# Output projection walked by halves of the tokens, with the second norm and the first dense products interleaved

## What is computed

```
for l in range(2):
    x = x + mod[2] * (concat(attention, conv, rwkv, fourier) @ w_out[l])   # the output projection
    h = modulate(rms_norm(x, norm2_w[l]), mod[3], mod[4])                  # the second norm
    if l == 0:   # dense block, 22 tiles of 128 hidden channels
        x = x + mod[5] * ((silu(h @ w1) * (h @ w3)) @ w2)
    else:        # router, top 2 of 8 experts
        x = x + mod[5] * moe_swiglu(h, router_w, w1, w3, w2)
```

## Time and profile before

| | |
|---|---|
| time, median of 2 runs | 2254.22 us (2253.96 to 2254.49) |
| the profiled execution: its time | 2271.23 us |
| its span | 2269.0 us, so 2.2 us lie around it |
| mean granted TensorE clock | 0.956 |
| TensorE busy | 2093.4 us, 92% |
| VectorE / ScalarE / GpSimd busy | 53% / 31% / 12% |

### The profile page before, as it was taken

One profiled execution on the slowest core, in us unless ns is written; L12 is line 12 of the kernel. 1 busy time (PEld: TensorE's weight loads), 2 busy tenths in 40 slices (PEclk: granted clock), 3 DMA queues, 4 the chain that ended last, 5 costly groups with the idle time before them and its releaser, 6 DMA issues.

```text
span 2269.0 us, 48183 instructions
## 1 busy us (share of the span) xinstructions
PE 2093.4 (92%) x20626; PEld 1798.4 (79%) x20626; DVE 1202.9 (53%) x2421; ACT 694.1 (31%) x1194; POOL 265.0 (12%) x377
## 2 busy tenths in 40 slices
PE   6999788889799999999899969888969999999996
PEld 3757577786599999999666757887749999899995
DVE  3458645544466422323456864545166666666664
ACT  3010323330422122121211142342045444544542
POOL 0000214520000000000000303551000110101110
PEclk8999869999899999999999978999989999999998
DMA  8253201001134322210435301000145666656666
GB/s 301 94 204 113 77 3 43 4 5 36 40 111 149 112 75 75 75 66 30 149 103 172 107 31 41 7 4 3 38 183 185 219 218 203 210 210 220 211 200 200
DMA packets 190652, 256.51 MB, mean 113 GB/s; under 512 B 9168, under 2 KB 141728, under 8 KB 190272
## 3 DMA queue, kind: packets, MB, share of 16 engines
q1 hardware_dynamic: 185456, 237.32, 30.2%
q0 software_dynamic: 4992, 16.13, 2.9%
HBM read 239.26 MB, written 16.78 MB: 113 GB/s over the span
## 4 chain that ended last, share of the span: by engine, by line
PE 82%; DVE 8%; issue 3%; ACT 3%; DMA 2%; SPq 1%; POOL 1%; DVEq 0%; ACTq 0%; POOLq 0%
PE bank L970 41%; PE bank L961 9%; PE bank L1241 9%; PE bank L1483 6%; PE bank L944 3%; PE bank L1120 3%; PE bank L1209 2%; PE bank L1226 2%; PE bank L1197 1%; PE bank L931 1%; DMA ring<-in_moe_w 1%; DVE arena L2393 1%; ACT arena L1660 1%; DVE rms L1943 1%; DMA arena<-in_mod_w 1%
## 5 line engine op out<-in xcount | busy, mean ns | idle before, releaser
L970 PE MATMUL bank<-g_hi,w_hi 128*128 128x224 f32 (+1 forms) x1376 | 392.8, 285 | 10.2 <-issue 6.4
L970 PE MATMUL bank<-g_hi,w_lo 128*128 128x224 f32 (+1 forms) x1376 | 391.4, 284 | 0.0
L970 PE MATMUL bank<-g_lo,w_hi 128*128 128x224 f32 (+1 forms) x1376 | 391.2, 284 | 0.0
L2131 DVE TENSOR_TENSOR w_lo<-ring,w_hi 128x1024 fp32r<-128x1024 f32 x192 | 232.2, 1223 | 133.9 <-ACT w_hi L1901 133.7
L1241 PE MATMUL bank<-arena 64*64 64x64 f32 (+1 forms) x8640 | 261.6, 226 | 32.1 <-issue 19.0
L1241 PEld LDWEIGHTS bank<-arena 64*64 64x64 f32 x8640 | 245.9, 134 | 47.0 <-issue 25.3
L970 PEld LDWEIGHTS bank<-g_hi,w_hi 128*128 128x128 f32 x1376 | 264.6, 192 | 12.2 <-issue 7.2
L970 PEld LDWEIGHTS bank<-g_lo,w_hi 128*128 128x128 f32 x1376 | 264.6, 192 | 0.2
L970 PEld LDWEIGHTS bank<-g_hi,w_lo 128*128 128x128 f32 x1376 | 264.5, 192 | 0.0
L1901 ACT ACTIVATE w_hi<-ring 128x1024 fp32r<-128x1024 f32 x192 | 202.3, 1060 | 129.5 <-PE bank L970 113.8
L970 PE MATMUL bank<-h_hi,w_hi 128*128 128x320 f32 x704 | 221.2, 314 | 11.5 <-DVE h_lo L2496 11.5
(11 more groups left out here) (296 smaller groups left out, 2929.8 us busy)
## 6 DMA issues: line engine op xcount, KB each, us to landing
ring<-in_moe_w SPq DMA_DIRECT2D x100, 1024.0 KB, 7.1
arena<-in_mod_w SPq DMA_DIRECT2D x40, 1024.0 KB, 5.3
ring<-in_ffn_w SPq DMA_DIRECT2D x30, 1024.0 KB, 7.4
ring<-in_w_in SPq DMA_DIRECT2D x16, 1024.0 KB, 7.5
ring<-in_w_out SPq DMA_DIRECT2D x8, 1024.0 KB, 8.6
ring<-in_mod_w SPq DMA_DIRECT2D x8, 1024.0 KB, 6.2
ring<-in_dft SPq DMA_DIRECT2D x4, 1024.0 KB, 7.4
ring<-in_w_in SPq DMA_DIRECT2D x4, 896.0 KB, 11.0
```

The costliest lines, as they stand in the source:

```text
L970: ins = mm(out, lhs[x], rhs[y], start=(first and i == 0), stop=(last and i == 2))
L2131: v.tensor_tensor(dst[1], src, f32(dst[0]), ALU.subtract).then_inc(s_lo2, 1)
```

## The change

The projection is walked by halves: 8 tiles of half 0, then 8 tiles of half 1. The second norm is done per half. Sums of squares of half 0 (one row-group sum and one fold) stand on TensorE between the tiles of half 1; root, inversion, scaling, shift, and in layer 0 `h_hi` and `h_lo` of half 0, stand on ScalarE and VectorE between the residuals of half 1. In layer 0 the first eight product groups of the dense block (chunks 0 and 1) are ordered half 0 first, with the sums of half 1 behind the first of them, and `w_lo` of chunks 0 and 1 stands ahead of the norm of half 1. The mod sums, takes and folds of the dense block each move one chunk later. In layer 1 the router's parts are made per half, and the early transposes stand between them. The line numbers shift: L970 becomes L995, L1483 becomes L1519, L2048 becomes L2170, L2606 becomes L2713, L1974 becomes L2096.

```diff
@@ project on TensorE, both layers
-                square_parts(2, l, 2 * l + 2)
-                sum_squares(2, l)
+                for h in range(2):
+                    for dt in range(KT):
+                        g = (dt, h)
+                        if g in early:
+                            end(project(g, (4, 5)))
+                            continue
+                        if g == (4, 0):
+                            wait_item(pe, ("wout", l, 1))
+                        banks[g] = psum[order.open(pe, ("out", l, dt, h))]
+                        end(project(g, (0, 1, 2, 3, 6, 7, 4, 5)))
+                        if g == (0, 1):
+                            second_sums(l, 0)
+                        elif g == (1, 1):
+                            sum_part(2, l, 0)
...
@@ dense on TensorE
             def dense():
+                for n, (f, q, h) in enumerate(FIRST_UPS):
+                    dense_up(0, f, q, h)
+                    if n == 0:
+                        second_sums(0, 1)
+                        sum_part(2, 0, 1)
                 for p, (_, nf) in enumerate(DENSE_PARTS):
-                    for f in range(nf):
-                        n = chunk_no[(p, "up", f)]
-                        pe.wait_ge(s_lo, n + 1)
...
-                        if p == 0 and f > 0:
-                            mod_sub(1, f - 1)
+                                dense_up(p, f, q, h)
+                        if p == 0:
+                            mod_sub(1, f - 2)
...
@@ norm2 and loop over chunks on ScalarE
+                for k in range(KT):
+                    square(1, k)
+                    if 2 <= k < 6:
+                        shift(0, 2 * k - 4)
+                        shift(0, 2 * k - 3)
+                    if l == 0 and k == 6:
+                        dense_split(0)
+                if l == 0:
+                    dense_split(1)
+                    silu(0, 0, 0)
+                else:
+                    b = take(("rpart", l, 0))
+                    end(ac(rt_part[:, 0:HALF], b[:, 0:HALF], ACT.Copy))
+                root(2, l, 1)
...
                     for n, (p, kind, i) in enumerate(chunks):
-                        if n + 1 < len(chunks):
+                        if 0 < n < len(chunks) - 1:
                             dense_split(n + 1)
...
@@ norm2 on VectorE
+                    elif dt == 6:
+                        low(0, 6)
+                        low(0, 7)
+                        if l == 0:
+                            dense_split(0)
+                if l == 0:
+                    dense_split(1)
+                b = take(("sp2", l, 1))
+                end(v.tensor_copy(rs[:, HALF:TOK], b[:, 0:HALF]))
+                invert(2, l, 1)
+                chain.settle()
+                for k in range(KT):
+                    scale(k, HALF_SEGS[1])
+                    if k >= 2:
+                        low(1, k - 2)
+                low(1, KT - 2)
+                low(1, KT - 1)
...
@@ loop over chunks on VectorE
+                    for h in range(2):
+                        for i in range(2):
+                            gated(0, i, h)
                     for n, (p, kind, i) in enumerate(chunks):
-                        if n + 1 < len(chunks):
+                        if 0 < n < len(chunks) - 1:
...
+                            if u >= 2:
+                                for h in range(2):
+                                    gated(p, i, h)
                             ve.wait_ge(s_ghi, u + 1)
                             v.tensor_tensor(dg[1][:, i, :], sil[:, u % 2, :], f32(dg[0][:, i, :]), ALU.subtract).then_inc(s_glo, 1)
...
+                        if 1 < n <= SUB_FIRST + 1:
+                            mod_take(1, n - 2)
                         if 0 < n <= SUB_FIRST:
-                            mod_take(1, n - 1)
-                        if n < SUB_FIRST:
-                            mod_sums(1, n)
+                            mod_sums(1, n - 1)
```

More of the change, by code:

```diff
@@ new lines, in _ @@
+                for g in early:
+                    banks[g] = psum[order.open(pe, ("out", l, g[0], g[1]))]
+                    project(g, (0, 1, 2, 3, 6, 7))
+                for ct in range(2):
+                    for h in range(2):
+                        order.wait_emptied(pe, ("gup", l, ct, h))
+                for h in range(2):
+                    for dt in range(KT):
+                        g = (dt, h)
[10 more added lines that the diff above has]
+                            sum_part(2, l, 0)
@@ L1553, in _ @@
                             end(ins)
-                for h in range(2):
-                    order.wait_emptied(pe, ("ss2", l, h))
                 if l == 0:
@@ L1633, in take, with norm1 @@
                 return psum[order.bank(name)]
-            def norm(l, which, then=None):
-                if l == 0 and which == 1:
+            def norm1(l):
+                if l == 0:
                     for j in range(NT):
@@ L1666, in in_evac, with silu, by_token @@
+            def silu(p, i, h):
+                u = DENSE_PARTS[p][0] + i
+                b = take(("du", p, i, 0, h))
+                end(ac(sil[:, u % 2, HALF * h:HALF * (h + 1)], b[:, 0:HALF], ACT.Silu))
+            def by_token(tiles):
+                for j, q in tiles:
+                    if q == 0:
+                        b = take(("ht", j, q))
+                        end(ac(h_tok[:, j, 0:512], b[:, :], ACT.Copy))
             def in_evac(l, tiles):
@@ L1849, in _ @@
                                 act.wait_ge(s_glo, u - 1)
-                            for h in range(2):
-                                b = take(("du", p, i, 0, h))
-                                end(ac(sil[:, u % 2, HALF * h:HALF * (h + 1)], b[:, 0:HALF], ACT.Silu))
+                                for h in range(2):
+                                    silu(p, i, h)
                             if i == 0 and p > 0:
@@ L1929, in take, with scales @@
                 return psum[order.bank(name)]
-            def norm(l, which, then=None):
-                b = take((f"sp{which}", l, 1))
-                end(v.tensor_copy(rs[:, HALF:TOK], b[:, 0:HALF]))
-                if which == 1:
-                    first_mods(l)
+            def scales(l, which):
                 t = 24 * (which - 1) + 8
@@ L1940, in norm, with invert, norm1 @@
                                                  in1=w[:, :, None].broadcast_to([P, KT, 2]), op0=ALU.add, op1=ALU.mult))
+            def invert(n, l, h):
+                order.wait_emptied(ve, (f"ss{n}", l, h))
+                chain.did(v.reciprocal(rs[:, HALF * h:HALF * (h + 1)], rs[:, HALF * h:HALF * (h + 1)]))
+            def norm1(l):
+                b = take(("sp1", l, 1))
+                end(v.tensor_copy(rs[:, HALF:TOK], b[:, 0:HALF]))
+                first_mods(l)
+                scales(l, 1)
@@ L1951, in norm, with scale @@
-                    ins.then_inc(s_hmul, 1)
-                    if then and k >= 2:
-                        then(k - 2)
-                if then:
-                    then(KT - 2)
-                    then(KT - 1)
+                    scale(k, SEGS)
+            def scale(k, segs):
+                for vec, lo, hi in segs:
+                    ins = v.scalar_tensor_tensor(out=hT[:, k, lo:hi], in0=xT[:, k, lo:hi], scalar=amul[:, k, vec:vec + 1],
+                                                 in1=rs[:, lo:hi], op0=ALU.mult, op1=ALU.mult)
+                    if vec == 0:
+                        chain.did(ins)
+                ins.then_inc(s_hmul, 1)
@@ L2489, in _, with by_token @@
                         end(v.tensor_tensor(yT[:, ct, cols], b[:, 0:HALF], yT[:, ct, cols], ALU.mult))
-                for dt in range(KT):
-                    for h in range(2):
-                        end(residual(take(("out", l, dt, h)), h, dt, 16))
-                def low(k):
-                    ve.wait_ge(s_hhi, k + 1)
-                    v.tensor_tensor(hc[1][:, k, :], hT[:, k, :], f32(hc[0][:, k, :]), ALU.subtract).then_inc(s_hlo, 1)
-                if l == 0:
-                    dense_split(0)
-                    norm(l, 2, low)
-                else:
-                    norm(l, 2)
-                if l == 1:
+                norm2(l)
+                if l == 1:
+                    def by_token(tiles):
+                        for j, q in tiles:
+                            if q == 1:
+                                b = take(("ht", j, q))
+                                end(v.tensor_copy(h_tok[:, j, 512:1024], b[:, :]))
+                    by_token(HT_EARLY)
                     three = lambda x: x[:, :, None].broadcast_to([P, NT, NE])
```

273 lines of the change are left out of this document (149 added, 124 removed).

## The result

The changed kernel takes 2286.43 us (median of 2 runs, 2281.60 and 2291.26) against 2254.22 before. The measured ratio is 1.0109, with a 95% interval of 1.0068 to 1.015: slower by 1.1%, less than the 2% that this measurement can surely tell from no change, but by its interval a loss. The two medians shown, divided, give 1.0143 (32.2 us); from which runs the smaller ratio comes isn't known, and the interval holds both. The forecast was 2280, range 2262 to 2291. The profiled execution is the longer of the two: 2291.26 us, span 2289.4, which is 20.4 us over the span of before.

The account below looks back on a forecast made before the run. TensorE, busy 92% of the span, was taken as the bound, with the load ring near the path. Layer 0's 30.8 us loss less layer 1's 5.2 gain put 2254.2 + 25.6 at 2280 us, range 2262 to 2291.

Parts of the forecast that it names:

- What bounds the kernel: Whole kernel: TensorE busy 92% of the span; the ring is near the path, `w_lo` of chunk 4 3.7 us ahead.
- Part 1: Layer 0 up to chunk 2: norm of half 1 covered, new stand of 3.6 us, chunk 2 starts 14.1 us sooner.
- The clock at small stands: Layer 0, TensorE's slower clock behind the small stands: 1 us at chunk 2 and 1 us at chunk 10.
- Part 2: Layer 0's ring: loads wait for later mod sums, stands of 10.6 us at chunks 4, 6, 8; layer 0 loses 30.8.
- Down(0,1), the bound at 2290: Dense block, layer 0: if down(0,1) lands with up(1,0) after 13.7 us, not 7.9, 5.8 us more, 2290.
- Part 3: Layer 1, projection end to first expert: router part copied 4.9 us earlier, 5.2 gained in all, carried through the gather.
- The sum: Whole kernel: 30.8 us lost in layer 0 less 5.2 gained in layer 1, 2280 us, 1.1% slower.
- (a): Dense block, layer 0: ring not on the path, only parts 1 and 3 count, 2237 us; chance 0.1.
- (b): Layer 0's projection: VectorE falls behind on half 0, `w_lo` of chunk 0 late by 5 to 10, 2287 us; chance 0.08.
- (c): Less loss: one of layer 0's three stands short, or layer 1 gains more, 2262 to 2267 us; chance 0.07.

Follow-up runs that it names:

- queue_order: Changed kernel with three swaps on SP's queue, each next dense load ahead of the modulation item beside it; ratio 0.996, median 2250.31 us.
- filled: Changed kernel with 40 added products, results overwritten, in TensorE's two waits of layer 1; 44.05 us from projection end to first expert product.
- trimmed: Changed kernel with 9 and 13 added products in layer 1's two waits; 42.63 us from projection end to first expert product.
- the shift alone: Kernel before with only the three modulation sums, takes and folds one chunk later; ratio 1.0199.
- the best version: Changed kernel with sum 0 in VectorE's idle time, later sums at old chunks, chunk 2's high and low parts earlier; ratios 0.9913 and 0.9903.

## Why the prediction was right

**What bounds the kernel.** Right. The 3.7 us of margin that the ring had before was the number that mattered, and no share of the page showed it.

**Part 1, gain to chunk 2.** Forecast 14.1, measured 14.5. Its pieces: the projection 2.1 longer against 1.9; TensorE 0.9 ahead of the first dense product against 0.97; 3.6 at chunk 2 against 3.6 (from 619.2 to 622.8). The norm of half 1 is covered, as said. The table loads cost nothing; each takes 1.28 us in the trace of the changed kernel, at 590.9, 592.6 and 605.7. The one at 590.89 starts 0.02 us behind ScalarE's instruction before it, and the silu behind it starts at 592.19. So the Trainium skill's 2.66 us for a switch with its drain ("ScalarE: Activation LUTs", What ACT_TABLE_LOAD costs) is not what these rows show.

**The clock at small stands.** Mis-sized, downwards. I took 1 us at chunk 2; chunk 2 took 15.85 instead of 14.18, 1.7. I took 1 at chunk 10; the stretch from there is 284.57 us against 295.80 x 20 / 21 = 281.7, 2.9. In the window of the stand at chunk 2 the granted clock was still 0.99, and the slow products came behind it (0.50 from 624 to 626). I had tied the price to the length of the stand, and a stand of 3.6 us can cost as much as one of 10: the three long ones cost 2.9, 2.1 and 1.7, and behind the same stand of 3.6 chunk 2 took 15.68 and 15.83 us in two other runs (`queue_order`, `filled`) and 17.12 in a third (`trimmed`), so 1.5 to 2.9 over 14.18.

**Part 2, the ring.** Right in mechanism, place and nearly in size. SP issues at the chunk's end + 8.38 (8.4); the pair lands 13.05, 13.1 and 12.8 us later, at the short end of the 13.0 to 14.3 from which I took 13.7. So the stands are 10.1 at most and not 10.6, with 19.8 to 20.1 us of wait on ScalarE ahead of each of these `w_hi`. The 2.0 us between forecast and measurement at chunk 10 are a balance: the three landings are 2.2 shorter, part 1 gave 0.4 more, and the step to chunk 10 (19.1 us from the end of chunk 8, not 19.4) 0.3; against that the slow products at chunks 2 to 8 cost 0.8 more in all than I took, and the way from landing to products 0.1. The queue alone undoes it, and the shift alone makes it.

**Down(0,1), the bound at 2290.** It landed in 7.7 us, 771.96 to 779.66, though up(1,0) was issued within 4.3 us behind it: the small value. The Trainium skill's rule ("DMA: Bandwidth & Descriptors", Queues, rings and completion order), each transfer engine takes a ring's descriptors in order, agrees with that; the trace agrees.

**Part 3, layer 1.** The step that failed in size. Forecast 5.2, measured 2.1 in the profiled execution, and 3.2 in the mean of six (50.3 - 45.2 - 1.9). Up to VectorE's copy of the last router part it was right (4.9 forecast; 19.17 us from the end of the projection before, 12.09 after, less 1.9, is 5.2). Behind it I carried the gain through with the durations of before, "since that chain is one line from here", and TensorE's part of that line ran at 1.2 GHz. Before, the granted clock had fallen too (0.50 from 1656 to 1660, behind a wait of 6.35 us), but the router parts, fed to TensorE one by one, came behind that wait and took the slow time, and it was 1.00 again from 1664 on, well ahead of the position products at 1670.26. The change spreads this work over two halves with waits of 2.3, 0.6 and 3.2 us between. With the first and the last filled the gain is 6.0 (50.3 - 42.4 - 1.9), close to the 4.9 + 1.2 that the forecast had called possible.

**The sum.** +27.8 and 2.9 for the clock at chunk 10, less 3.2, makes +27.5 by the profiles (+30.0 with the layer 1 of the profiled execution and the small rest), against +25.6 forecast. The ratio puts it at +24.6, between 15 and 34. So that the forecast came within 2 us by the profiles is in part luck: the two clock terms and layer 1, mis-sized to the loss's side by 0.7, 1.9 and 2.0 to 3.1 us, are partly cancelled by the shorter landings. By the medians the loss is 32.2 us, 6.6 over the forecast and still inside its range.

**Rivals.** (a) at 2237, the sums in VectorE's idle time, didn't occur; the best version built it. It gained 20 and 22 us by its ratios where (a) had 17.5, but it also takes away the 3.6 us at chunk 2, which (a) kept. VectorE did have that idle time, and the changed kernel doesn't use it. (b) didn't occur: `w_lo` of chunk 0 was in time but for 1 us. (c) didn't either: all three stands were whole.

## What to carry to other kernels

A step that is moved on one engine may be the one that frees a buffer, and a queue that issues in order then holds back every load behind it, also those that have nothing to do with the step: read which queue entry waits for the moved step, and reorder the queue together with it. Ask of a hidden load by how many microseconds it was hidden (here 3.7) before moving anything by a whole iteration (15). And look for the idle time into which the displaced work would fit before giving it someone else's slot: here 10.8 us stood free beside a sum of 6.2.

## What the runs showed of the hardware that was not expected

The price of TensorE's clock doesn't follow the length of the stand: behind a stand of 3.6 us the next 96 products took 1.5 to 2.9 us longer in four runs, behind stands of 10 us 1.7 to 2.9 in the changed kernel. It also fell with no long stand ahead: with waits of 2.3, 0.6 and 3.2 us and work between them it was 0.68 from 1676 to 1680, 0.89 in the next 4 us and 0.53 from 1684 to 1688. That costs others: VectorE waited for transposes at half speed. Products whose results are thrown away kept it at 1.00, and were worth 2.8 us in the mean in a stretch of 45 where they ended with the wait; where they ran 2.1 us past it, 1.1.

Executions of the same code differ by up to 10 us (first residual at 523.1 to 533.5) by the time they reach the change, in a kernel of 2254; a window of the mixers shows the granted clock at 0.59 in one execution and at 0.91 in another. Differences between profiles were therefore taken only from a point that both share.
